# Delta stage of a hybrid encoder step: 16-row diagonal blocks solved on VectorE through DRAM, three joins on TensorE, fronts two tiles ahead

## The reference

```python
decay = exp(where(tri, gc[..., :, None] - gc[..., None, :], -inf))
k_beta = k * beta[..., None]
lower = where(strict, einsum('bhid,bhjd->bhij', k_beta, k) * decay, 0.0)
a = eye(c) + lower
rhs = concatenate([v * beta[..., None], k_beta * exp(gc)[..., None]], -1)
sol = triangular_solve(a, rhs, lower=True, unit_diagonal=True)
u, w = sol[..., :DV_B], sol[..., DV_B:]
v_new = u - einsum('bhcd,bhde->bhce', w, state)
attn = where(tri, einsum('bhid,bhjd->bhij', q, k) * decay, 0.0)
o = einsum(q * exp(gc)[..., None], state) + einsum(attn, v_new)
new_state = state * exp(g_last)[..., None] + einsum(k * exp(g_last - gc)[..., None], v_new)
```

## Time and profile before

| | us |
|---|---|
| median of three timed runs | 3119.41 |
| lowest and highest | 3111.07, 3119.99 |
| the profiled execution's own time | 3119.69 |
| its span in the trace | 3117.9 |
| TensorE busy | 2966.4 |
| VectorE busy | 1664.0 |
| ScalarE busy | 845.5 |
| GpSimd busy | 390.0 |
| mean granted TensorE clock | 0.972 |

### The profile page before, as it was taken

One profiled execution on the slowest core, in us unless ns is written; L12 is line 12 of the kernel. 1 busy time (PEld: TensorE's weight loads), 2 busy tenths in 40 slices (PEclk: granted clock), 3 DMA queues, 4 the chain that ended last, 5 costly groups with the idle time before them and its releaser, 6 DMA issues. The chain is left out here.

```text
span 3117.9 us, 45731 instructions
## 1 busy us (share of the span) xinstructions
PE 2966.4 (95%) x16871; PEld 2787.6 (89%) x16871; DVE 1664.0 (53%) x3002; ACT 845.5 (27%) x1510; POOL 390.0 (13%) x297
## 2 busy tenths in 40 slices
PE   6999999999989899999798999879989999999998
PEld 6999999999889699999687899779889999999997
DVE  5444455554341588997344555267745555444445
ACT  4111111111232345552564233121131111111112
POOL 0000000000000155451310555020000000000000
PEclk9999999999999999999898999689999999999999
DMA  4111111111111122222102101242111111111111
GB/s 143 41 40 40 40 40 40 40 40 45 38 33 34 36 84 74 80 93 94 53 15 57 45 27 31 100 146 91 50 54 41 40 40 40 40 52 48 41 34 61
DMA packets 213831, 170.38 MB, mean 55 GB/s; under 512 B 30281, under 2 KB 194681, under 8 KB 213730
## 3 DMA queue, kind: packets, MB, share of 16 engines
q1 hardware_dynamic: 206674, 140.63, 15.3%
q10 hardware_dynamic: 4752, 18.94, 1.6%
q0 software_dynamic: 2304, 9.44, 0.8%
HBM read 136.61 MB, written 32.31 MB: 54 GB/s over the span
## 5 line engine op out<-in xcount | busy, mean ns | idle before, releaser
L502 DVE TENSOR_TENSOR ffn_prod<-ffn_silu,ffn_p_up 128x384 f32<-128x384 f32 x132 | 73.1, 554 | 769.2 <-ACT ffn_silu L422 769.2
L484 DVE SCALAR_TENSOR_TENSOR x<-ffn_p_down,x 128x512 f32<-128x512 f32 x738 | 474.8, 685 | 1.3 <-PE ffn_p_down L153 1.3
L153 PE MATMUL ffn_p_gate<-ffn_hT_hi,ffn_g_hi 128*128 128x384 f32 x1056 | 357.1, 338 | 17.9 <-ACT ffn_silu L422 10.8
L153 PE MATMUL ffn_p_gate<-ffn_hT_hi,ffn_g_lo 128*128 128x384 f32 x1056 | 355.6, 337 | 0.0
L153 PE MATMUL ffn_p_gate<-ffn_hT_lo,ffn_g_hi 128*128 128x384 f32 x1056 | 355.5, 337 | 0.0
L153 PE MATMUL ffn_p_up<-ffn_hT_hi,ffn_u_hi 128*128 128x384 f32 x1056 | 353.6, 335 | 0.0
L153 PE MATMUL ffn_p_up<-ffn_hT_hi,ffn_u_lo 128*128 128x384 f32 x1056 | 353.0, 334 | 0.0
L153 PE MATMUL ffn_p_up<-ffn_hT_lo,ffn_u_hi 128*128 128x384 f32 x1056 | 352.8, 334 | 0.0
L422 ACT ACTIVATE ffn_silu<-ffn_p_gate 128x384 f32<-128x384 f32 x132 | 64.9, 492 | 870.9 <-PE ffn_p_up L153 870.9
L153 PE MATMUL ffn_p_down<-o_c_hi,o_t_lo 128*128 128x512 f32 x756 | 295.3, 391 | 0.0
L153 PE MATMUL ffn_p_down<-o_c_lo,o_t_hi 128*128 128x512 f32 x756 | 294.8, 390 | 0.0
(11 more groups left out here) (363 smaller groups left out, 5421.1 us busy)
## 6 DMA issues: line engine op xcount, KB each, us to landing
ffn_raw_g<-in_ffn_w_gate SPq DMA_DIRECT2D x44, 512.0 KB, 5.0
ffn_raw_u<-in_ffn_w_up SPq DMA_DIRECT2D x44, 512.0 KB, 6.1
ffn_raw_d<-in_ffn_w_down SPq DMA_DIRECT2D x44, 512.0 KB, 3.5
h_raw<-in_w_in SPq DMA_DIRECT2D x32, 512.0 KB, 3.8
projected_d<-sp_stage ACTq DMA_DIRECT2D x20, 576.0 KB, 2.8
conv_d<-sp_stage ACTq DMA_DIRECT2D x12, 576.0 KB, 3.2
dl_qkv<-conv_d SPq DMA_DIRECT2D x9, 768.0 KB, 4.8
mg_gate_a<-projected_d POOLq DMA_DIRECT2D x8, 576.0 KB, 3.9
```

The lines of the kernel that those rows point to most:

```text
L153: mm = nc.tensor.matmul(out, stationary(k)[a], moving(k)[b], start=(start and at == 0 and i == 0), stop=(stop and 3 * at + i == n - 1))
L484: nc.vector.scalar_tensor_tensor(out=xs, in0=p_down[(NO * q + o) % 4][:], scalar=0.5, in1=xs, op0=ALU.mult, op1=ALU.add).then_inc(added, 1)
L502: nc.vector.tensor_tensor(prod[:, slot], silu[:, slot], p_up[slot][:, 0:TG], ALU.mult).then_inc(prod_done, 1)
```

## The change

Tile 0 keeps its six joins. For the tiles 1 to 7 the levels below 16 rows leave TensorE: `levels_of` gives levels 4, 5 and 6, and for the decode tile none. In their place the 16-row diagonal blocks of low are inverted on VectorE. The 4 heads have 32 such blocks, one on each of 32 partitions. SP stores low to DRAM and loads the 32 blocks from there (`to_blocks`). `solve` goes row by row: 15 multiplies and 15 subtracts, each waiting for the one before, then a turned copy. SP stores the result and the turned result to DRAM and loads both back with the rows on 128 partitions (`from_blocks`). `expand` spreads them over the diagonal with a mask: they are the X and Y from which the joins start.

Fronts are prepared two tiles ahead (`front_of`): step 0 prepares tiles 1 and 2, step n the tile n+2, one third of the front beside each join. So vb, kbg, kdec, qTe, attn and `below` have three buffers. kbg and kdec move from GpSimd (two instructions) to ScalarE (`scale_k`, eight instructions of one head each). The loop over pairs of tiles is written out. The end of tile 7 comes after the last join.

The core of the diff (lines that are gone are in the functions above, except at the top):

```diff
-LEVELS_P, LEVELS_S = 7, 4
+LEVELS_P = 7
+BLOCK, BLOCK_LEVEL = SEQ_S, 4
+BLOCK_STEP = BLOCK * HB * P + BLOCK
...
+def levels_of(n):
+    return range(1 if n == 0 else BLOCK_LEVEL, LEVELS_P) if n < NTP else range(0)
...
-        below = s.sbuf("below", [P, 2, LEVELS_P, HB, P])
-        X, vb, kbg, kdec, qTe, attn, Y, wT = (s.sbuf(n, [P, 2, HB, P]) for n in (
-            "X", "vb", "kbg", "kdec", "qTe", "attn", "Y", "wT"))
+        below_first = s.sbuf("below_first", [P, LEVELS_P, HB, P])
+        below = s.sbuf("below", [P, 3, LEVELS_P - BLOCK_LEVEL, HB, P])
+        X, Y, wT = (s.sbuf(n, [P, 2, HB, P]) for n in ("X", "Y", "wT"))
+        vb, kbg, kdec, qTe, attn = (s.sbuf(n, [P, 3, HB, P]) for n in ("vb", "kbg", "kdec", "qTe", "attn"))
...
+        block_low, solved, product, unit = (s.sbuf(n, [NB, BLOCK, BLOCK]) for n in ("block_low", "solved", "product", "unit"))
+        turned = s.sbuf("turned", [NB, BLOCK, BLOCK])
+        packed = s.sbuf("packed", [P, 2, 2, HB, BLOCK])
...
+        def front_of(n, at):
+            m = n + 2 if n else 1 + at // 3
+            return (m, at % 3) if m < NT else (None, at % 3)
...
+            def to_blocks(m):
+                sp.wait_ge(low_ready, m + 1)
+                sp.dma_start(lower_d[m % 2, 0:P * HB * P].rearrange("(p h c) -> p h c", h=HB, c=P), low[:]).then_inc(
+                    low_stored, 16)
+                sp.wait_ge(low_stored, 16 * m)
+                if m >= 2:
+                    sp.wait_ge(solve_done, m - 1)
+                own = lower_d[m % 2].rearrange("(b r) -> b r", r=BLOCK_STEP)[:, 0:BLOCK * HB * P].rearrange(
+                    "b (i h c) -> h b i c", h=HB, c=P)
+                for h in range(HB):
+                    sp.dma_start(block_low[h * P // BLOCK:(h + 1) * P // BLOCK], own[h][:, :, 0:BLOCK]).then_inc(blocks_in, 16)
+            def from_blocks(m):
+                sp.wait_ge(solve_done, m)
+                for i, part in enumerate((solved, turned)):
+                    sp.dma_start(solved_d[m % 2, i].rearrange("(b r) -> b r", b=NB), part[:].rearrange(
+                        "b i j -> b (i j)")).then_inc(solve_stored, 16)
+                sp.wait_ge(solve_stored, 32 * m)
+                if m >= 3:
+                    sp.wait_ge(expanded, m - 2)
+                for i in range(2):
+                    sp.dma_start(packed[:, m % 2, i], solved_d[m % 2, i].rearrange(
+                        "(h b i j) -> (b i) h j", h=HB, i=BLOCK, j=BLOCK)).then_inc(packed_in, 16)
...
+            load(2)
+            to_blocks(1)
+            for n in range(NT):
+                if n + 3 < NT:
+                    load(n + 3)
+                if n + 1 < NT:
+                    from_blocks(n + 1)
+                if n:
+                    store(n - 1)
+                if n + 2 < NT:
+                    to_blocks(n + 2)
...
+            def step(n):
+                last = len(levels_of(n)) - 1
+                for at in range(last + 1):
+                    m, third = front_of(n, at)
+                    z(n, at, 0)
+                    if at:
+                        x(n, at - 1, 1)
+                    z(n, at, 1)
+                    if m:
+                        (rows_and_k, turn_hats, grams_q)[third](m)
+                    y(n, at, 0)
+                    y(n, at, 1)
+                    if n:
+                        (new_values, outputs, state)[third](n - 1)
+                    if at < last:
+                        x(n, at, 0)
+                    if m and third < 2:
+                        (q_and_v, grams_k)[third](m)
+                weights(n)
...
+            def expand(m):
+                dve.wait_ge(packed_in, 32 * m)
+                if m >= 2:
                     dve.wait_ge(v_done, m - 1)
...
+                for i, part in enumerate((X, Y)):
+                    ins = nc.vector.tensor_tensor(
+                        part[:, m % 2].rearrange("p h (b j) -> p h b j", j=BLOCK),
+                        packed[:, m % 2, i].rearrange("p h (a j) -> p h a j", a=1).to_broadcast([P, HB, P // BLOCK, BLOCK]),
+                        const.rest[:, SAME_S, :].rearrange("p (a b j) -> p a b j", a=1, j=BLOCK).to_broadcast(
+                            [P, HB, P // BLOCK, BLOCK]), ALU.mult)
+                ins.then_inc(expanded, 1)
+            steps = [0]
+            def then(ins):
+                steps[0] += 1
+                ins.then_inc(solve_step, 1)
+                dve.wait_ge(solve_step, steps[0])
+            def solve(m):
+                if m >= 2:
+                    dve.wait_ge(solve_stored, 32 * (m - 1))
+                then(nc.vector.tensor_copy(solved[:], unit[:]))
+                dve.wait_ge(blocks_in, 64 * m)
+                for j in range(BLOCK - 1):
+                    shape = [NB, BLOCK - 1 - j, j + 1]
+                    then(nc.vector.tensor_tensor(product[:, j + 1:, 0:j + 1], block_low[:, j + 1:, j:j + 1].to_broadcast(shape),
+                                                 solved[:, j:j + 1, 0:j + 1].to_broadcast(shape), ALU.mult))
+                    then(nc.vector.tensor_tensor(solved[:, j + 1:, 0:j + 1], solved[:, j + 1:, 0:j + 1],
+                                                 product[:, j + 1:, 0:j + 1], ALU.subtract))
+                nc.vector.tensor_copy(turned[:], solved[:].rearrange("b i j -> b j i")).then_inc(solve_done, 1)
...
+            def step(n):
+                last = len(levels_of(n)) - 1
+                for at in range(last + 1):
+                    m, third = front_of(n, at)
+                    if at:
+                        keep_x(n, at - 1, 1)
+                    keep_y(n, at, 0)
+                    keep_y(n, at, 1)
+                    if m and third == 0:
+                        gaps(m)
+                        hat_k(m)
+                    if at < last:
+                        keep_x(n, at, 0)
+                    if m:
+                        (hat_q_and_v, lower, attend_in_tile)[third](m)
+                    if third == 0 and n + 1 < NT and at == max(0, last - 2):
+                        solve(n + 1)
+                if n:
                     next_state(n - 1)
+                if n + 1 < NT:
+                    expand(n + 1)
...
+            def scale_k(m):
+                act.wait_ge(khat_ready, m + 1)
+                if m >= 3:
+                    for p in range(2):
+                        act.wait_ge(w_done[p], m - 2)
+                    act.wait_ge(s_done, m - 2)
+                for part, factor, ready in ((kbg, c_key, k_scaled), (kdec, c_last, k_faded)):
+                    for h in range(HB):
+                        ins = nc.scalar.activation(part[:, m % 3, h, :], khat[:, h, :], ACT.Copy,
+                                                   scale=factor[:, m, h:h + 1])
+                    ins.then_inc(ready, 1)
...
+            def step(n):
+                for at in range(len(levels_of(n))):
+                    m, third = front_of(n, at)
+                    keep_z(n, at, 0)
+                    keep_z(n, at, 1)
+                    if m and third == 0:
+                        row_exp(m)
+                    if n and third == 0:
                         keep_values(n - 1)
...
+                    if m and third == 0:
+                        exps(m)
+                    if m and third == 1:
+                        keep_hats(m)
+                    if n and third == 1:
+                        keep_outputs(n - 1)
+                    if m and third == 2:
+                        scale_k(m)
...
+            def front(m):
+                if m + 1 < NT:
                     spread_g(m + 1)
                 pool.wait_ge(qT_kept, m + 1)
                 pool.wait_ge(e_row_done, m + 1)
...
+                if m >= 3:
+                    pool.wait_ge(o_done, m - 2)
+                nc.gpsimd.tensor_tensor(qTe[:, m % 3], qT[:], e_row[:], ALU.mult).then_inc(q_scaled, 1)
                 pool.wait_ge(low_ready, m + 1)
...
+                if m >= 3:
                     for p in range(2):
...
+                        pool.wait_ge(y_done[p], joined[m - 2])
+                def blocks(of, i):
+                    nc.gpsimd.tensor_tensor(of, low[:], for_heads(masks[:, i, :], HB), ALU.mult).then_inc(b_made, 1)
+                if m == 0:
+                    blocks(below_first[:, 0], 0)
+                    blocks(below_first[:, 1], 1)
+                    pool.wait_ge(b_made, 1)
+                    nc.gpsimd.tensor_tensor(X[:, 0], for_heads(const.ident[:], HB), below_first[:, 0],
+                                            ALU.subtract).then_inc(x_first, 1)
+                    for i in range(2, LEVELS_P):
+                        blocks(below_first[:, i], i)
+                elif m < NTP:
+                    for at, i in enumerate(levels_of(m)):
+                        blocks(below[:, m % 3, at], i)
                 pool.wait_ge(attn_ready, m + 1)
...
+                nc.gpsimd.tensor_tensor(attn[:, m % 3], attn[:, m % 3], for_heads(
```

(61 more changed lines are left out.)

338 lines of the change are left out of this document (135 added, 203 removed).

## The result

The changed kernel took 3125.65 us (median of 8 executions, 3123.39 to 3129.34), the kernel before, beside it on the same chip, 3117.68 (8, 3110.26 to 3119.99). The ratio is 1.0032, 95% interval 1.0021 to 1.0043: some 10 us longer, where I forecast 3125 us and +5.4. A second comparison, run later with the experiments, gave 3125.04 against 3111.46, 1.0045 (1.0027 to 1.0063). Medians and ratios leave out two slow executions, 3691 us of the kernel without rows and 5849 us of the one with rows spread and the mask late. The time came out as forecast.

What follows compares the result with a forecast made beforehand. TensorE, busy 95% of the span, was taken as the bound in the steady tiles. Tile 0 +14.0, tiles 1 to 6 +2.1, tiles 7 and 8 -10.7 sum to +5.4 us on 3119.7: 3125 us, range 3107 to 3144.

Steps and rivals of the forecast that it cites:

- The solve and the stand: VectorE's row solve at the first join's end takes 7.8 us; TensorE stands 6.5 us before y(n,1,1).
- rival of a longer solve: Solve longer than 7.8 us, deciding from 8.3; at 9.7 us the kernel takes 3140 us; chance 0.24.
- 8.5 us saved per tile: TensorE in tiles 1 to 7: 76 records removed at 0.111 us each, 8.5 us per tile.
- The clock after the stand: TensorE restarts at the lower clock level after the 6.5 us stand, costing 2.0 us per step.
- at the step's end: Clock fall after TensorE's 2.15 us stand at the step's end: 4 in 10 of 1.7 us, 0.7.
- The rival in which the clock holds: Clock holds or falls beside the path; tiles 0 to 7 keep 2.0 to 2.7 us each; 3105 us; chance 0.20.
- ScalarE ends last at the step's end: Eight scaled copies and the first wT copy on ScalarE end after VectorE's expand; next z starts at 26.15 us.
- Tile 0: Tile 0 keeps six joins and prepares tiles 1 and 2, with solve, stand and clock: +14.0 us.
- Tiles 7 and 8: The last prompt tile and the decode tile together go from 42.6 to 31.9 us, -10.7.
- The way through DRAM: From solve to expand, two stores and two loads take 7.5 us, hidden in steady steps, on the path only in tile 7.
- The rival of a slow DRAM: The way back takes 13 us instead of 7.5: +17 us, 3142 us; chance 0.06.
- both stretches at nothing: Before 1717 and after 1961 us the change leaves the work as it is, but for small edits counted as nothing.

Runs made afterwards that it cites:

- kernel without rows: Changed kernel with the 30 row operations of each solve left out, copies, DRAM and joins kept: 3054.2 us, ratio 0.9807 to the kernel before.
- rows spread and the mask late: Changed kernel with the 30 row operations in three places and GpSimd's attn masking held until expand is done: 3084.0 us, ratio 0.9905 to the kernel before.
- fillers: Changed kernel with 26 identity products put on TensorE ahead of y(n,1,1): 3107.3 us, ratio 0.9982 to the kernel before.
- in three parts with the mask late and SyncE's order turned: Changed kernel, rows in three places, attn masked after expand, low stored before packed loads, output stored last: 3078.9 us, ratio 0.9887 to the kernel before.
- the run with every second row: Changed kernel with only rows 0, 2, 4, ... of each solve computed, 16 of 30 operations: 3092.3 us, ratio 0.993 to the kernel before.

## Why the prediction was right, point by point

**The solve and the stand: right.** Forecast 7.8 us from the earlier trace rows, measured 7.5 (1858.17 to 1865.71), operations 0.19 to 0.25 apart; a stand of 6.5, measured 6.26; y(n,1,1) 15.5 us after z at full clock, measured 15.28 in tile 4. The rival of a longer solve (from 8.3 us on) fell. Leaving rows out shows that they are what turns 8.5 us saved per tile into none; spreading the same rows shows that it is their place in the queue.

**The clock after the stand: right; at the step's end: too low.** The first was priced at 2.0 and took 1.6 in tile 4 (half of 3.1 us), 1.9 on the mean of the six tiles (13.13 us from y(n,1,1) to the next z, and 11.25 with fillers). The second I gave 4 in 10, 0.7; it came in 5 of 6 steps, 1.4 to 1.6 us each (y starts 16.7 to 16.9 after z, instead of 15.28), 1.3 on the mean. Together the clock costs 3.2 us a step for 2.7. The rival in which the clock holds is answered by the filler products: 18 us faster, the 20 I had given it.

**ScalarE ends last at the step's end: wrong.** This is the step that failed. Its eight copies went as priced (0.30 apart for 0.29), but I took expand at 1.3 us, from products of 0.68 us that read one operand from PSUM (dl_front). It took 2.2, because GpSimd's attn mask runs at that moment and both engines read two SBUF operands. VectorE so ended last, 0.49 us behind ScalarE. (My terms for VectorE's end, 22.8 + 0.6 + 1.1 + 1.3, make 25.8 and not 25.65; ScalarE would still have been last.) At full clock y(n,1,1) to the next z took 11.25 us for 10.65 forecast, 0.6 more, and this 0.49 is most of it; the head took 15.28 for 15.5. The 0.9 by which a step missed (29.7 for 28.85, +7.2 us over six tiles for +2.1) is thus 0.4 of work and 0.5 of clock. These shares are worked out from the steps; that the mask makes expand longer is shown by the run that moves it.

**Tile 0: +17.9 for +14.0,** and +14.2 when the changed kernel ran again: the same code, 48.0 and 44.3 us. What makes the 3.7 us between the two executions was not tried.

**Tiles 7 and 8: right,** 32.6 for 31.9, -9.9 for -10.7. The measured stage is +15.2 us for +5.4.

**The way through DRAM: hidden, right; its price too high.** The DMA issues of the changed kernel's stage, columns as in the earlier trace rows:

```profile
dl_packed<-solved_d SPq DMA_DIRECT2D x16, 32.0 KB, 2.0
...
solved_d<-dl_solved SPq DMA_DIRECT2D x8, 32.0 KB, 1.5
```

512 packets of 64 bytes landed in 2.0 us, where I took 3.8 from a row of 512-byte packets: the way is some 4.9 us, not 7.5, just under my lower bound of 5. The rival of a slow DRAM is out.

**Why the total still fits.** The stage is 9.8 us longer than forecast, and the span only +6.1. The stage began 4.3 us sooner (1712.75 for 1717.08), after work that the change leaves alone, and the decode tail, the same code too, took 43.7 us (to the load of sb_o) for 48.6, at a higher clock. The windows of before and then of the changed kernel, two halves of that tail:

```profile
1960.90:1985.00 24.10, 22.75 (x101) 20.18 (x102) 3.68 (x7) 1.17 (x2) 0.00 (x0) 0.54 0.04 12
1985.00:2009.50 24.50, 18.57 (x65) 13.13 (x64) 9.83 (x30) 0.58 (x1) 0.00 (x0) 0.64 0.32 96
```
```profile
1971.70:1995.00 23.30, 21.89 (x104) 19.35 (x105) 4.32 (x10) 1.17 (x2) 0.00 (x0) 0.58 0.05 15
1995.00:2015.50 20.50, 14.48 (x62) 10.15 (x61) 9.11 (x28) 0.59 (x1) 0.00 (x0) 0.75 0.38 115
```

I had left both stretches at nothing. A hit of 0.65 us on 3125 is therefore luck in size, though not in sign: the medians of the two comparisons differ by +8 and +13.6 us, the stage alone by +15.2 and +10.9. In the second profile of the changed kernel the stage began at 1719.44, 2.4 us later than before, and the tail took 40.4 us. What makes those stretches vary was not tried.

## What to carry to other kernels

A chain of small dependent operations is cheap by its sum and dear by its place: what counts is which result is queued behind it on its engine. Here the same 30 operations cost some 71 us in one block and, in three parts with the mask late and SyncE's order turned, some 25 (3078.9 against 3054.2). When work moves to an engine, look not only at its busy share but at what the neighbour engine does in that microsecond, and price the clock that a new stand brings as a term of its own.

## What the runs showed of the hardware

- VectorE operations with two SBUF operands and GpSimd's products take turns, whole instructions at a time: 0.68 us became 1.61, and a row operation 0.19 us became 1.27, as long as the GpSimd instruction that it met. VectorE operations with a PSUM operand ran beside GpSimd at their usual length (in the changed kernel attn, from dl_front, 0.68 us at 1846.98, while GpSimd's blocks ran from 1844.72 for 3.74). The Trainium skill, SBUF — State Buffer, section on SBUF's two separate sides, says the same of the port pair that these two engines share, an exclusive lock held for the instruction; I had not weighed it, and the trace agrees.
- After stands of 3.0 us TensorE came back at either of its levels (in the run with every second row), after 6.3 us at the lower every time. Identity products kept it at the upper one (2.4 GHz).
- The decode tail, untouched in all runs, took from 40.4 us (no rows; changed again) to 49.7 (rows spread, mask late): a stretch of one profiled execution can move by 9 us, as much as this change moved the whole kernel (8 to 14 us). In the two tails shown above the granted clock moved with it.
